# Norm chains in halves shared crosswise by two engines, and first panels that take the two token groups in turn

## The reference

```python
def rmsnorm(x, g):
    xf = x.astype(F32)
    y = xf * lax.rsqrt(jnp.mean(xf * xf, axis=-1, keepdims=True) + EPS)
    return (y * g.astype(F32)).astype(x.dtype)

def trunk_layer(x, cvec, l, P, hg_lower, cache):
    mod = jax.nn.silu(cvec) @ P['w_mod'][l] + P['b_mod'][l]
    mod = mod.reshape(cvec.shape[0], 1, N_MOD, D_MODEL)
    g = P['norm_g'][l]
    h = rmsnorm(x, g[0]) * (1.0 + mod[:, :, 1]) + mod[:, :, 0]
    m, ctx = token_mixers(h, l, P, hg_lower, cache)
    x = x + mod[:, :, 2] * rmsnorm(m, g[1])
    h = rmsnorm(x, g[2]) * (1.0 + mod[:, :, 4]) + mod[:, :, 3]
    if l % 2 == 0:
        f = swiglu(h, P['w_ffn_gu'][l // 2], P['w_ffn_down'][l // 2])
    else:
        f = moe(h, P['w_router'][l // 2], P['w_exp_gu'][l // 2], P['w_exp_down'][l // 2])
    x = x + mod[:, :, 5] * rmsnorm(f, g[3])
    return x, ctx
```

## Time and profile before

| | |
|---|---|
| median of 3 runs | 1771.74 us (1771.68 to 1772.72) |
| the profiled execution | 1773.81 us, of which its span is 1772.0 |
| TensorE busy | 1683.4 us, 95% of the span |
| DVE busy | 1257.9 us, 71% |
| ACT busy | 987.8 us, 56% |
| chain that ended last | PE 91%, DMA 3%, ACT 2%, DVE 2% |
| granted TensorE clock, mean | 0.977 of full speed |

### The profile page before, as it was taken

The page is one execution under the profiler, slowest core; times in us unless marked ns, Lnnn a source line. Parts: engine busy times, 40 slices in busy tenths (PEclk is TensorE's granted clock), DMA queues, the critical chain, the costliest instruction groups (busy, mean ns, idle before and its releaser), DMA issues.

```text
span 1772.0 us, 20649 instructions
## 1 busy us (share of the span) xinstructions
PE 1683.4 (95%) x8358; PEld 1377.0 (78%) x8358; DVE 1257.9 (71%) x1087; ACT 987.8 (56%) x969; POOL 125.4 (7%) x87
## 2 busy tenths in 40 slices
PE   4999999989999799999877999999999999999996
PEld 2778888767778677888766888888888888888885
DVE  2555889644443645698754888888888888888884
ACT  4434533543333633543343777777777777777773
POOL 1100242000000110133100000000000000000000
PEclk8999999999999899999996999999999999999998
DMA  9864444288753576434352999999999999999981
GB/s 399 334 269 172 151 176 149 107 333 292 276 190 115 229 293 224 184 143 148 149 206 88 354 359 342 354 362 338 360 341 359 338 360 343 354 359 338 362 328 43
DMA packets 55969, 470.64 MB, mean 266 GB/s; under 512 B 6368, under 2 KB 6416, under 8 KB 8768
## 3 DMA queue, kind: packets, MB, share of 16 engines
q1 hardware_dynamic: 53136, 460.22, 70.3%
q0 software_dynamic: 2736, 9.05, 1.3%
HBM read 465.05 MB, written 4.19 MB: 265 GB/s over the span
## 4 chain that ended last, share of the span: by engine, by line
PE 91%; DMA 3%; ACT 2%; DVE 2%; issue 1%; POOL 0%; SPq 0%; POOLq 0%; ACTq 0%; DVEq 0%
PE ps L1054 27%; PE ps L1056 26%; PE ps L1055 26%; PE ps L1023 2%; PE ps L1309 2%; PE ps L1127 2%; PE ps L1225 1%; DMA ring<-in_w_in 1%; DMA u<-in_w_mod 1%; PE ps L1343 1%; PE ps L1100 1%; PE ps L1217 1%; DMA ring<-in_w_mod 0%; PE ps L1571 0%; DVE ring_lo L1907 0%
## 5 line engine op out<-in xcount | busy, mean ns | idle before, releaser
L1907 DVE TENSOR_TENSOR ring_lo<-ring,w_hi 128x2048 fp32r<-128x2048 f32 x297 | 680.0, 2292 | 161.8 <-ACT w_hi L791 161.0
L1054 PE MATMUL ps<-ring_lo,h_both 128*128 128x512 f32 x1520 | 610.2, 401 | 20.6 <-DVE h_both L1820 12.8
L791 ACT ACTIVATE w_hi<-ring 128x2048 fp32r<-128x2048 f32 x297 | 567.7, 1914 | 92.0 <-PE ps L1056 91.8
L1054 PEld LDWEIGHTS ps<-ring_lo,h_both 128*128 128x128 f32 x1520 | 287.9, 189 | 88.3 <-issue 30.6
L1056 PE MATMUL ps<-w_hi,h_both 128*128 128x512 f32 x896 | 352.2, 393 | 0.0
L1055 PE MATMUL ps<-w_hi,h_both 128*128 128x512 f32 x896 | 351.2, 392 | 0.0
L776 ACT ACTIVATE ring_lo<-ring 128x2048 fp32r<-128x2048 f32 x90 | 172.1, 1915 | 200.1 <-PE ps L1056 198.4
L1830 DVE TENSOR_TENSOR ring_lo<-ring,ring_lo 128x2048 fp32r<-128x2048 f32 x74 | 177.7, 2407 | 117.2 <-ACT ring_lo L776 116.5
L1055 PE MATMUL ps<-ring_lo,h_both 128*128 128x512 f32 x624 | 244.6, 392 | 0.0
L1056 PE MATMUL ps<-ring_lo,h_both 128*128 128x512 f32 x624 | 244.6, 392 | 0.0
L1056 PEld LDWEIGHTS ps<-w_hi,h_both 128*128 128x128 f32 x896 | 169.4, 189 | 37.2
(11 more groups left out here) (282 smaller groups left out, 1509.3 us busy)
## 6 DMA issues: line engine op xcount, KB each, us to landing
ring<-in_w_ff SPq DMA_DIRECT2D x297, 1024.0 KB, 4.9
ring<-in_w_in SPq DMA_DIRECT2D x36, 2048.0 KB, 7.9
u<-in_w_mod SPq DMA_DIRECT2D x21, 2048.0 KB, 9.8
ring<-in_w_br SPq DMA_DIRECT2D x6, 2048.0 KB, 7.8
ring<-in_w_o SPq DMA_DIRECT2D x4, 2048.0 KB, 7.8
ring<-in_w_mod SPq DMA_DIRECT2D x3, 2048.0 KB, 16.7
out<-state_out POOLq DMA_DIRECT2D x4, 512.0 KB, 4.7
x_sb<-in_x SPq DMA_DIRECT2D x1, 1024.0 KB, 10.6
```

The lines of the kernel that those rows point to most:

```text
L791: A(w_hi[p], ring[slab_slot(n)][:, p * UNIT:(p + 1) * UNIT], ACT.Copy).then_inc(hi_ready[p], 1)
L1054: mm(out, a_hi, b_lo, start=start, stop=False, skip_group_check=True)
L1907: V.tensor_tensor(ring_lo[slot][:, part], ring[slot][:, part], w_hi[p].bitcast(F32), ALU.subtract)\
```

## The change

1. Each chain goes in two halves of 512 columns. For the rows DVE takes half 0 and ACT half 1 of either group; the transposed half 0 is read by ACT and half 1 by DVE; `input_hi` and `input_lo` go half by half. In the norm of a sum DVE scales half 1 while ACT squares half 0, and then they swap. Residuals are two operations with a semaphore each, and x is squared half by half. The two sums of squares meet in the mean square.
2. The first panel of a layer (`first_panel`) and the first tile of the channel mixer in layer 0 take the groups in turn, and in each half of the weights all high by high products come first, then high by low, then low by high (`by_pass`), each behind its own wait.
3. At the boundary of the layers the queues of ACT and DVE are reordered: the norm 0 of group 0 in layer 1 comes before the norm 3 of group 1 in layer 0 is finished; group 1 follows behind group 0's `h` and behind unit 1 of the weights. POOL does all these norms before its five DMA issues.
4. y is stored in four DMAs. Six semaphores of the start are merged into two.

```diff
+NORMS = [(0, 0, 0), (0, 0, 1), (0, 1, 0), (0, 2, 0), (0, 1, 1), (0, 2, 1), (0, 3, 0), (1, 0, 0), (0, 3, 1), (1, 0, 1),
+         (1, 1, 0), (1, 2, 0), (1, 1, 1), (1, 2, 1), (1, 3, 0), (1, 3, 1)]
...
             def squares_x(l, n, g):
...
+                for half, ready in ((0, x_half), (1, x_new)):
+                    if n == 0 and l == 0:
+                        act.wait_ge(s_x, 16)
+                    else:
+                        act.wait_ge(ready, sum_at(l, 1, g) if n else sum_at(l - 1, 3, g))
+                    ins = A(xn[:, g, columns(half)], x_sb[:, g, columns(half)], ACT.Square, scale=D ** -0.5,
+                            accum_out=ss[:, 2 * g + half:2 * g + half + 1])
+                ins.then_inc(sq_ready, 1)
...
+            def rows(l, n, g):
+
+                act.wait_ge(sq_ready, norm_at(l, n, g))
+                act.wait_ge(rs_ready, norm_at(l, n, g))
+                A(xn[:, g, columns(1)], x_sb[:, g, columns(1)], ACT.Copy, scale=rs[:, g:g + 1]).then_inc(xn1_ready, 1)
...
             def squares_sum(l, n, g):
 
+                unused = h_lo[:, g].rearrange("p k t -> p (k t)")
                 act.wait_ge(*summed(l, n, g))
-                A(h_lo[:, g].rearrange("p k t -> p (k t)"), ps[:, 2 * g:2 * g + 2, :].rearrange("p b c -> p (b c)"),
-                  ACT.Square, accum_out=ss[:, g:g + 1]).then_inc(sq_ready, 1)
+                A(unused[:, columns(0)], ps[:, 2 * g, :], ACT.Square, scale=D ** -0.5,
+                  accum_out=ss[:, 2 * g:2 * g + 1]).then_inc(sq_half, 1)
+                act.wait_ge(post_half, sum_at(l, n, g))
+                A(unused[:, columns(1)], ps[:, 2 * g + 1, :], ACT.Square, scale=D ** -0.5,
+                  accum_out=ss[:, 2 * g + 1:2 * g + 2]).then_inc(sq_ready, 1)
...
             for l in range(L):
-                for g in range(2):
-                    squares_x(l, 0, g)
-                rows(l, 0)
+                squares_x(l, 0, 0)
                 if l == 0:
+                    squares_x(l, 0, 1)
+                else:
+                    squares_sum(l - 1, 3, 1)
+                rows(l, 0, 0)
+                if l == 0:
+                    rows(l, 0, 1)
                     copy_mod(0, ps[:, 0:1, :])
                     mix_split(0, 0)
                 act.wait_ge(mod_ready, l + 1)
                 turn_read(l, 0, (0,))
                 input_hi(l, 0, (0,))
+                if l:
+                    squares_x(l, 0, 1)
+                mix_split(l, 1)
+                if l:
+                    rows(l, 0, 1)
                 turn_read(l, 0, (1,))
                 input_hi(l, 0, (1,))
-                for m in range(1, SLOTS):
-                    mix_split(l, m)
+                mix_split(l, 2)
                 decay_tables(l)
...
+            def by_pass(out, a, g, first, hi, lo, hi_made, lo_made, a_made, start, stop):
+
+                a_hi, a_lo = a
+                pe.wait_ge(*a_made[0])
+                pe.wait_ge(*hi_made)
+                for k in range(4):
+                    mm(out, a_hi[:, g, first + k, :], hi[:, k, :], start=start and k == 0, stop=False, skip_group_check=True)
+                pe.wait_ge(*lo_made)
+                for k in range(4):
+                    mm(out, a_hi[:, g, first + k, :], lo[:, k, :], start=False, stop=False, skip_group_check=True)
+                pe.wait_ge(*a_made[1])
+                for k in range(4):
+                    ins = mm(out, a_lo[:, g, first + k, :], hi[:, k, :], start=False, stop=stop and k == 3, skip_group_check=True)
+                return ins
...
+            def first_panel(l):
+
+                pe.wait_ge(mod_ready, l + 1)
+                for g in range(2):
+                    if l and g:
+                        turn_rows(l, 0, (1,))
+                    for half in range(2):
+                        key, _, hi, count = mix_unit(l, half)
+                        lo = ring_lo[plan[key][0]][:, half * UNIT:(half + 1) * UNIT]
+                        hi, lo = (v.rearrange("p (k c) -> p k c", k=4) for v in (hi, lo))
+                        ins = by_pass(ps[:, g, :], (h_hi, h_lo), g, 4 * half, hi, lo, (mix_hi, count + 1), mix_lo_made(l, half),
+                                      input_made(l, 0, g, half), half == 0, half == 1)
+                        if g == 1:
+                            ins.then_inc((mix_half, win_done)[half], 1)
...
             def gate_sum(l, n, g):
 
-                dve.wait_ge(gb_read, sum_at(l, n, g))
-                V.tensor_tensor(pair(xn[:, g, :]), ps[:, 2 * g:2 * g + 2, :], pair(gate_copy(l, n, g)), ALU.mult).then_inc(post_read, 1)
+                for half, done in ((1, post_half), (0, post_read)):
+                    if half:
+                        dve.wait_ge(gb_read, sum_at(l, n, g))
+                        dve.wait_ge(*summed(l, n, g))
+                    else:
+                        dve.wait_ge(sq_half, sum_at(l, n, g))
+                    V.tensor_tensor(xn[:, g, columns(half)], ps[:, 2 * g + half, :], gate_copy(l, n, g)[:, columns(half)], ALU.mult)\
+                        .then_inc(done, 1)
...
             for l in range(L):
                 mean_square(l, 0, 0)
                 if l:
-                    residual(l - 1, 3, 1)
-                rows(l, 0)
-                mean_square(l, 0, 1)
+                    gate_sum(l - 1, 3, 1)
+                    mean_square(l - 1, 3, 1)
+                else:
+                    mean_square(l, 0, 1)
+                rows(l, 0, 0)
                 if l == 0:
+                    rows(l, 0, 1)
                     link(read_mod(0, 2, 0))
                     modulation(0, 0, 2, mod_ready, 1)
                 turn_read(l, 0, (0,))
                 if l == 0:
                     mix_split(0, 0)
                 input_lo(l, 0, (0,))
+                if l:
+                    residual(l - 1, 3, 1)
+                mix_split(l, 1)
+                if l:
+                    mean_square(l, 0, 1)
+                    rows(l, 0, 1)
                 turn_read(l, 0, (1,))
                 input_lo(l, 0, (1,))
-                for m in range(1, SLOTS):
-                    mix_split(l, m)
+                mix_split(l, 2)
                 decay_tables(l)
...
+                gate_sum(l, 3, 0)
                 mean_square(l, 3, 0)
-                gate_sum(l, 3, 0)
                 residual(l, 3, 0)
-                mean_square(l, 3, 1)
-                gate_sum(l, 3, 1)
+            gate_sum(L - 1, 3, 1)
+            mean_square(L - 1, 3, 1)
             residual(L - 1, 3, 1)
```

More of the change, by code:

```diff
@@ L551, in _ @@
                 sp.wait_ge(q, 16 * L)
[L552 removed]
+            sp.wait_ge(s_yout, 64)
         @block.gpsimd
@@ L562, in power, with norms @@
                 pool.tensor_tensor(out, in_, con_("half")[:, 0:1].broadcast_to([P, n]), ALU.pow).then_inc(done, 1)
-            def norms(l, order):
-                for n, g in order:
+            def norms(first, end):
+                for l, n, g in NORMS[first:end]:
                     pool.wait_ge(ms_ready, norm_at(l, n, g))
@@ L755, in input_hi @@
                 for g in groups:
-                    act.wait_ge(ht_dve, 4 * l + n + g + 1)
-                    act.wait_ge(ht_act, 4 * l + n + g + 1)
-                    A(h_hi[:, g], h32[:, g], ACT.Copy).then_inc(h_hi_ready, 1)
+                    for half, read in ((0, ht_act), (1, ht_dve)):
+                        act.wait_ge(read, rows_at(l, n, g))
+                        blocks = slice(4 * half, 4 * half + 4)
+                        A(h_hi[:, g, blocks], h32[:, g, blocks], ACT.Copy).then_inc(h_hi_ready, 1)
             def mix_split(l, m):
@@ L986, in _ @@
                     mix_split(1, 0)
-                    for g in range(2):
-                        squares_sum(0, 3, g)
+                    squares_sum(0, 3, 0)
                 else:
@@ L1042, in turn_rows @@
             def turn_rows(l, n, groups=(0, 1)):
[L1044 removed]
                 for g in groups:
[L1046 to L1050 removed]
+                    for half, ready, done in ((0, xn_ready, xt_half), (1, xn1_ready, xt_done)):
+                        pe.wait_ge(ready, rows_at(l, n, g))
+                        for k in range(4):
+                            at = half * 512 + k * P
+                            ins = nc.tensor.transpose(ps[:, 4 + 2 * g + half, k * P:(k + 1) * P], xn[:, g, at:at + P], ident)
+                        ins.then_inc(done, 1)
             def product(out, a_hi, a_lo, b_hi, b_lo, start, stop):
@@ L1818, in input_lo @@
                 for g in groups:
-                    dve.wait_ge(h_hi_ready, input_count(l, n, g))
-                    V.tensor_tensor(h_lo[:, g], h32[:, g], h_hi.bitcast(F32)[:, g], ALU.subtract).then_inc(h_lo_ready, 1)
+                    for half in range(2):
+                        dve.wait_ge(h_hi_ready, input_count(l, n, g, half))
+                        blocks = slice(4 * half, 4 * half + 4)
```

(7 more changed lines are left out.)

133 lines of the change are left out of this document (59 added, 74 removed).

## The result

The changed kernel takes 1775.05 us (median of 20 runs, 1773.31 to 1777.37), the kernel before beside it 1772.28 (20 runs, 1771.4 to 1774.06): a ratio of 1.0016, 95% interval 1.001 to 1.0023. That is 2.8 us slower, inside what I called no change (3.5 us). It lies inside the whole range (1768.0 to 1777.0), but at the edge of the forecast's own (1770 to 1775), and nearer to rival A (1775.4) than to the forecast (1772.3). With the 0.5 by which the median of before moved the forecast is 1772.8, 2.2 short. All ratios here are of runs in the fast state; one run of e1 (2148.07 us, at a mean granted clock of 0.746) is not in them. The profiled execution took 1774.89, of which 1773.1 is the span.

The account below looks back on a forecast made before the run. TensorE was taken as the bound, busy 1683.4 of 1772.0 us. Terms -1.8 + 2.1 + 1.0 - 1.2 + 0.5 = +0.6 on the profiled 1773.81, which lies 2.07 above the median, gave 1772.3 us; range 1768.0 to 1777.0.

Parts of the forecast that it names:

- no change: Whole kernel: a difference within about 0.2%, 3.5 us, can't be told from none; chance of this outcome 0.72.
- rival A: Layer boundary: short waits between 594 and 601.5 keep the clock down, +3.1 us, 1775.4 in all; chance 0.2.
- A's sign: Layer boundary: rival A holds if the granted clock between 597 and 604 is at the lower level.
- Start: Start of the kernel: TensorE begins at about 37.55, not 39.35; gain 1.8 us, from 1.6 to 2.5.
- What is late next is the decay tables: Start: the tables come 0.9 us behind unit 2, with 2 us to spare before unit 3 is wanted.
- Output: Output: group 1's second square waits for a DVE scaling behind group 0's residual halves; +0.5 us, 0 to +1.1.
- moves half as many bytes (about 0.6 less): Output: the last store, at 1768.8 instead of 1767.70, saves about 0.6 us by its smaller size.
- Second norm of layer 0: Layer 0: tile starts 3.4 us earlier, then idles until the slab lands, lower clock behind; +2.1 us, lower bound 0.
- rival B: Second norm of layer 0: the modulation slab isn't the floor, tile's 3.6 us gained, 2.1 not lost; 1766.6; chance 0.08.
- Boundary: Boundary of the layers: TensorE starts 4.7 us earlier, then waits give it back; +1.0 us, 0 to +4.1.
- Router: Second norm of layer 1: the router starts at 926.75 instead of 927.93; gain 1.2 us, 0 to 2.

Follow-up runs that it names:

- e1: Changed kernel with layer 0's modulation slab issued ahead of three weight parts: 1770.44 us, 0.9989 of the kernel before.
- e2: Changed kernel with the start's modulation slab issued ahead of the third weight slab: 1774.77 us, 1.0009 of the kernel before.
- e3: Kernel before with both slabs (start and layer 0) issued ahead, nothing else: 1771.63 us, ratio 0.9998.
- e4: Changed kernel with unit 1 of the weights split earlier on ACT and DVE at the layer boundary: 1774.83 us, 1.0014 of the kernel before.
- e7: Changed kernel with both slabs ahead, unit 1 early, a new DVE order at the output and two stores of y: 1765.37 us, ratio 0.9958.
- e10: e8 with idle transposes in all stops beside the norm chains: 1752.81 us, 0.9897 of the kernel before.
- e11: Kernel before with both slabs ahead (as e3) and all stops filled with idle transposes: 1759.88 us, ratio 0.9938.
- e12: e10 with every modulation slab issued ahead of the weights it stood behind: 1751.47 us, 0.9882 of the kernel before.
- e9: Changed kernel, unit 1 late, with idle transposes (36, 14, 10) in three boundary stops: 1775.66 us, 1.0023 of the kernel before.
- e8: e7 with idle transposes (36, 14, 10) in three boundary stops: 1762.35 us, 0.9947 of the kernel before.
- e6: Changed kernel with y stored in two stores of 512 KB, not four: 1776.61 us, 1.0023 of the kernel before.

## Why the prediction was right, and which two steps were not

No change was right, and so was the direction of each term, though the start's is close to nothing. By its number the result is nearer to rival A, but in the profiled execution A's sign is missing: the granted clock was 1.00 from 596 to 604. What the forecast was short by is two terms, the start (1.7 us) and the output (1.0), and the range was wide enough for both. The halves were costed rightly (the tile of layer 0 3.37 us earlier against 3.4, the first matmul of the boundary at 591.10 against 593.87 + 1.92 of shift, 4.7 earlier as forecast), and at three places of five the term is within 0.1.

**Start, "Gain 1.8".** The 1.8 were an honest count up to TensorE's first matmul and a little high (1.5). The failure is the sentence "What is late next is the decay tables". I looked at ACT and DVE for what comes next and not at the DMA, though the very next instruction behind the panel is a matmul on a slab, at 52.79 with no idle time in front of it, and at layer 0 I had just called a gain void for such a slab. A start without a wait says only that the slab was not late by then; how early it was has to be read from its issue and its time to landing. Here the slab had landed 0.45 us ahead of its use (31.19 + 21.1), so by this trace at most some 0.4 of the 1.8 could be kept; 0.1 was, since the slab landed 0.3 later in the changed kernel. e2 shows that the slab is the floor, and e3 that with the slow chain an earlier slab brings nothing.

**Output, "moves half as many bytes (about 0.6 less)".** The forecast of 1.1 us for the last residual half is exact (7.36 - 6.26). From the store's issue to the end it then took 0.44 us more, not 0.6 less. The 0.6 had no row; the only rows near it were two stores of 512 KB, and from one size no rate can be read. Measured, half the bytes save 0.1, and the last store pays for the three ahead of it (3.43 us to landing against 2.89).

**Second norm of layer 0** was right in sum by two errors that cancel. I had the tile partly at the lower clock and 4 us of idle time behind it; it ran at the full clock and the idle time was 5.42. The modulation starts when the slab lands, so neither matters. e1 and e3 show that the slab is the floor there, and that rival B (the gain of 3.6) is what happens without it: 3.3, up to the next slab.

**Boundary**: right in each wait (0.16 and 1.07 where I had 0.4 and 1.4, 1.82 where I had 1.8) and in the sum. Rival A didn't happen in the changed kernel's trace; the fall of the clock that it is about came one stop later in e1, e4 and e7. With the changed kernel's own order that is one execution of five, which the chance of 0.2 fits. Whether it is what spreads the runs of the changed kernel over 4.1 us (before: 2.7) can't be told from times alone.

**Router**: right (1.3 against 1.2).

Where did the gain go that such a rewrite could bring? About 6 us of it is real by the traces of e10 and e11, and e12 has some 2.7 more at the slabs. Two slabs took it back at two places, unit 1 and the clock at the third, and two small losses at the output were added.

## What to carry to other kernels

A stage that gets faster is worth nothing until the next thing that TensorE needs is early enough. So for every place ask for the landing of the next transfer, also where TensorE shows no wait for it today. A start without a wait has a slack, and the trace of before shows it if asked: issue plus time to landing, against the use (0.45 us at the start here). Issue order on the DMA queue cost nothing to change (e3), and it decided some 5 us here (e1).

A stop costs twice, by its length and by the half-rate matmuls behind it. Where a chain is shortened but TensorE still stops, look at the granted clock behind each stop in more than one execution; two edits that each do next to nothing (e4, e9) can be worth 4 us together (e8).

## What the runs showed of the hardware that was not expected

**Idle work pays.** 36, 14 and 10 transposes of the identity in three stops kept the granted clock at 1.00 (e8, from 575 to 603), where e7 without them had 0.50 from 579 to 589 and from 596 to 599.6. They give no work to DVE, ACT or the queues, and in all stops together they were worth 12.6 us in the changed kernel (e7 to e10, 1765.37 to 1752.81; 12.2 against the kernel before on each chip).

**Busy and yet slower.** In e12 TensorE shows no idle time from 920 to 930 and the granted clock fell, while it ran the router's 128x8 matmuls, the transposes behind them and then the idle ones. e10 has the same (0.50 from 920 to 930); in e11 the clock held over the same router matmuls and fell only at 930.8. All three have stops of 1.1 and 0.4 us just ahead, so it isn't shown whether these or the narrow matmuls brought it. The windows of e12:

```profile
915.00:920.00 5.00, 3.83 (x33) 3.60 (x33) 1.85 (x5) 3.51 (x6) 0.22 (x1) 1.00 1.01 418
920.00:925.00 5.00, 5.00 (x31) 5.00 (x31) 1.82 (x14) 0.21 (x1) 0.00 (x0) 0.64 0.78 328
925.00:930.00 5.00, 5.00 (x26) 5.00 (x25) 1.88 (x1) 1.88 (x1) 0.00 (x0) 0.50 0.00 2
```

**A late store.** ACT waits for the store of the state once in each layer, 2.38 to 2.40 us in 26 of the 28 cases of these traces, and 4.53 and 4.64 in the two others (e11 in layer 0, e12 in layer 1). Why is open; they cost the kernels 3.7 and 3.8 us, since TensorE stopped for 2.5 us behind it and then ran at the lower clock. The two rows, of e11 and of e12:

```profile
326.59 1.92 ACT L779 ACTIVATE w_hi<-ring 128x2048 fp32r<-128x2048 f32 x1 [4.53 <-DMA out<-state_out]
```

```profile
870.39 1.92 ACT L790 ACTIVATE w_hi<-ring 128x2048 fp32r<-128x2048 f32 x1 [4.64 <-DMA out<-state_out]
```

**Two paces of unchanged code.** A product step of an expert took 8.89 us between 1300 and 1390 in the traces of before, e3 and e6, and 8.87 in the eleven others; the granted clock was 1.00 in that stretch in all of them. From the router to the stop at 1749 that makes 1.3 us (821.07 before and 821.05 in e6, 819.81 in the changed kernel). It isn't the change, since e11 has the chains of before at the faster pace and e6 the new ones at the slower. What it is stays open.
